# A two-layer mixer kernel: where the inverse root of the latent key norm is turned into a column

## The reference, cut to what matters

```python
def _mla(c_q, c_kv, k_rope, positions, q_norm, kv_norm, wq_up, wkv_up, q_gain, k_gain):
    """c_q: (B,S,Q_RANK), c_kv: (B,S,KV_RANK), k_rope: (B,S,MLA_ROPE) shared over heads."""
    b, s, _ = c_q.shape
    q = (_rms_norm(c_q, q_norm) @ wq_up).reshape(b, s, MLA_HEADS, MLA_QK)
    kv = (_rms_norm(c_kv, kv_norm) @ wkv_up).reshape(b, s, MLA_HEADS, MLA_NOPE + MLA_V)
    k_nope, v = kv[..., :MLA_NOPE], kv[..., MLA_NOPE:]
...
    k = _rms_norm(k, k_gain).transpose(0, 2, 1, 3)
...
    return _from_heads(_causal_softmax_attention(q, k, v, MLA_QK ** -0.5))
...
def second_block(x, positions, ffn1_norm, ffn1_wi, ffn1_wo, mix_norm, w_in, b_in, ml_conv_w, ml_conv_b,
...
    for l in range(DEPTH_2):
        x = x + 0.5 * _swiglu(_rms_norm(x, ffn1_norm[l]), ffn1_wi[l], ffn1_wo[l])

        u = _rms_norm(x, mix_norm[l])
        c = _split_cols(u @ w_in[l] + b_in[l])
...
        y_mla = _mla(c['mla_cq'], c['mla_ckv'], c['mla_kr'], positions, mla_q_norm[l], mla_kv_norm[l],
                     mla_wq_up[l], mla_wkv_up[l], mla_q_gain[l], mla_k_gain[l])
...
        x = x + merged @ w_out[l]

        x = x + 0.5 * _swiglu(_rms_norm(x, ffn2_norm[l]), ffn2_wi[l], ffn2_wo[l])
    return x
```

## Time and profile before

| | |
|---|---|
| median of 3 runs | 2370.8 us (2369.12 to 2372.78) |
| the profiled execution | 2373.44 us |
| its span (first to last instruction) | 2371.6 us |
| PE busy | 2350.4 us, 99% of the span |
| PE in the chain that ended last | 97% of the span |
| mean granted TensorE clock | 0.997 |
| DVE, ACT, POOL busy | 49%, 41%, 56% of the span |

### The profile page before, as it was taken

One profiled execution on the slowest core, in us unless ns is written; L12 is line 12 of the kernel. 1 busy time (PEld: TensorE's weight loads), 2 busy tenths in 40 slices (PEclk: granted clock), 3 DMA queues, 4 the chain that ended last, 5 costly groups with the idle time before them and its releaser, 6 DMA issues.

```text
span 2371.6 us, 29650 instructions
## 1 busy us (share of the span) xinstructions
PE 2350.4 (99%) x11116; PEld 1917.7 (81%) x11116; DVE 1161.2 (49%) x1812; ACT 982.1 (41%) x1561; POOL 1319.6 (56%) x1589
## 2 busy tenths in 40 slices
PE   8999999999999999999999999999999999999999
PEld 8777788888888888777888888888887778888887
DVE  5895475422324432479636733333325795366330
ACT  4555644222223233566534432332346655343321
POOL 5784256655656654457345755555554573466554
PEclk9999999999999999999999999999999999999999
DMA  4322133333333333222132333333332122233333
GB/s 159 103 80 72 40 94 98 98 97 98 92 97 111 98 98 96 73 70 80 54 89 80 98 98 98 98 92 99 95 96 80 54 81 62 81 89 98 98 98 98
DMA packets 60862, 212.88 MB, mean 90 GB/s; under 512 B 6704, under 2 KB 8112, under 8 KB 60720
## 3 DMA queue, kind: packets, MB, share of 16 engines
q1 hardware_dynamic: 60576, 210.86, 29.5%
q10 hardware_dynamic: 144, 0.14, 0.0%
HBM read 208.87 MB, written 2.10 MB: 89 GB/s over the span
## 4 chain that ended last, share of the span: by engine, by line
PE 97%; ACT 1%; issue 1%; DVE 1%; POOL 0%; DMA 0%; SPq 0%; DVEq 0%
PE banks L741 96%; PE banks L1030 0%; PE banks L860 0%; POOL t L2046 0%; DMA t<-in_w 0%; ACT t L1715 0%; PE banks L910 0%; ACT t L1779 0%; PE banks L1087 0%; ACT t L1748 0%; ACT L2007 0%; ACT t L1751 0%; ACT t L1928 0%; ACT t L1746 0%; DVE t L1523 0%
## 5 line engine op out<-in xcount | busy, mean ns | idle before, releaser
L741 PE MATMUL banks<-t,t 128*128 128x512 f32 (+9 forms) x10836 | 2327.6, 386 | 18.1 <-ACT t L1735 5.8
L741 PEld LDWEIGHTS banks<-t,t 128*128 128x128 f32 (+2 forms) x10836 | 1886.6, 188 | 438.1 <-issue 51.5
L2046 POOL TENSOR_TENSOR t<-t,t 128x256 fp32r<-128x256 f32 x1544 | 1262.9, 849 | 1021.5 <-ACT t L1715 1012.7
L1715 ACT ACTIVATE t<-t 128x1024 fp32r<-128x1024 f32 x385 | 407.8, 1060 | 1075.7 <-issue 617.9
L1233 DVE TENSOR_TENSOR t<-banks,t 128x512 f32<-128x512 f32 x121 | 83.1, 687 | 171.3 <-PE banks L741 169.2
L1400 DVE TENSOR_TENSOR t<-banks,t 128x512 f32<-128x512 f32 x44 | 30.4, 691 | 184.1 <-PE banks L741 183.9
L1368 DVE SCALAR_TENSOR_TENSOR t<-banks,t 128x512 f32<-128x512 f32 x32 | 22.1, 692 | 155.4 <-PE banks L741 155.4
L1116 DVE SCALAR_TENSOR_TENSOR t<-t,t,t 128x512 fp32r<-128x512 f32 x64 | 52.9, 831 | 57.4 <-ACT t L1735 57.3
L1345 DVE TENSOR_TENSOR t<-t,t 128x512 fp32r<-128x512 f32 x68 | 70.1, 1031 | 2.3
L1735 ACT ACTIVATE t<-t,t 128x512 fp32r<-128x512 f32 x64 | 45.6, 715 | 55.6 <-DVE t L1368 49.1
L1374 DVE TENSOR_TENSOR t<-banks,t 128x512 f32<-128x512 f32 x24 | 16.6, 692 | 106.0 <-PE banks L741 106.0
(11 more groups left out here) (186 smaller groups left out, 1258.5 us busy)
## 6 DMA issues: line engine op xcount, KB each, us to landing
t<-in_w SPq DMA_DIRECT2D x386, 512.0 KB, 3.5
t<-in_xT SPq DMA_DIRECT2D x8, 256.0 KB, 6.0
out<-t SPq DMA_DIRECT2D x8, 256.0 KB, 4.4
t<-in_vbias SPq DMA_DIRECT2D x2, 384.0 KB, 4.0
t<-in_c SPq DMA_DIRECT2D x1, 576.0 KB, 8.4
t<-in_w SPq DMA_DIRECT2D x2, 256.0 KB, 4.0
t<-in_pos SPq DMA_DIRECT2D x2, 256.0 KB, 3.7
t<-in_dmask SPq DMA_DIRECT2D x4, 128.0 KB, 4.4
```

Of the source, the lines that this page charges most:

```text
L741: return pe.matmul(o, l, r, start=start, stop=stop, skip_group_check=True)
L1715: a.activation(whl[u % 2][:, 0:1024], wraw[u % 3][:, :], ACT.Copy).then_inc(*w_high.next(u))
L2046: p.tensor_tensor(hl[:, 1024:2048][:, c], wraw[u % 3][:, c], as_f32(hl[:, c]), ALU.subtract).then_inc(*w_low.next((u, q)))
```

## The change

The four thin matmuls of `cols` and their copy are taken out of `low_item`, where they followed the inverse roots, and are emitted between the last `qup` and the first `vup`. Instead of a bank of the item's own pair they take the next of the two banks of the dense products, so that the products behind them have the other bank of the two than before. `low_item` is done, for `until`, one step earlier. What is computed is the same.

```diff
                 put("low_sums", l)
                 yield "a", (t_attn, ("low_kv", l))
                 put("low_rs", l)
-                yield "t", (v_attn, ("low_kv", l))
-                put("cols", ("low", l), pair(slot)[0], 0, RKV, natural, rcol_t[:, 4:8], (v_attn, ("low_kv", l)))
                 sch.done.add(("low", l))
...
                 sch.pump()
+            put("cols", ("low", l), sch.bank(), 0, RKV, natural, rcol_t[:, 4:8], (v_attn, ("low_kv", l)))
             for t_ in range(2):
                 b = sch.bank()
                 g = len(groups)
```

## The result

The changed kernel takes 2378.36 us in the median of nine runs (2374.06 to 2379.40), the kernel before, run beside it, 2371.46 us (2367.62 to 2375.78). The ratio is 1.0027, with a 95% interval from 1.0019 to 1.0035: 6.4 us slower, a little over what a measurement of this kernel can tell from no change. The forecast was 4.0 us slower, and the likeliest class in it was "the same".

The account below looks back on a forecast made before the run. PE, busy 2350.4 of 2371.6 us, was taken to bound the kernel. Freed wait 0, thin matmuls 1.82, clock 2.2 and moved attention steps 0 made 4.0 us on 2370.8: 2374.8, range 2371.4 to 2378.2.

Parts of the forecast that it names:

- the same: Class of outcome: a time between 2366.1 and 2375.5 us, not told from no change; chance 0.66.
- The freed wait: Removing the wait behind line 1138 ahead of `kup` gains 0; at most 2.06 us a layer if the chain did not hold.
- The thin matmuls at the values: Four thin matmuls a layer ahead of `vup`, in PE's running stream, add 0.91 us a layer, 1.82 in all.
- The clock: At PE's restart the clock falls in both layers in nearly every run; 2.2 us in the first, 0 in the second.
- The attention steps among the gate products: Moved steps in the mixer, same matmuls and no PE wait: 0, half a microsecond a layer either way.
- The sum: For the whole kernel, 1.82 + 2.2 = 4.0 us, put on the median 2370.8: 2374.8.
- slower: Class of outcome: a time from 2375.5 us up; chance 0.32.
- second case: Clock at the restart as before, only the thin matmuls' cost left: 2372.6 us, chance 0.23.
- The clock does as it did: Rival: clock at the restart falls as often as before, only the thin matmuls cost, 1.8 us: 2372.6; chance 0.23.
- the early keys pay: Rival: the earlier `kup` pulls its successors forward, both waits of 2.06 us go: 2368.5; chance 0.05.
- The clock falls at the values too: Rival: thin and narrow matmuls at the values lower the clock, 1.7 us a layer more: 2378.2; chance 0.17.

Follow-up runs that it names:

- e1: The kernel before, its order kept, with the thin matmuls and their copy left out: 2373.92 us, ratio 1.0010.
- e3: The changed kernel with 12 unread 512-column matmuls behind the first key projection, in PE's long wait: 2374.26 us, ratio 1.0008 to the kernel before.
- e2: The kernel before with the thin matmuls and copy moved ahead of the values, banks exchanged, all else in its old order: 2375.41 us, ratio 1.0018.
- e9: The kernel before with 16 unread full fp32 128x128 matmuls in one block in each mixer's last gate products: 2380.27 us, ratio 1.0039.
- e10: The kernel before with 16 unread full fp32 128x128 matmuls a layer, one behind each of 16 gate steps: 2377.96 us, ratio 1.0031.
- e11: As e10, but each spare matmul writes 64 output rows in place of 128: 2391.02 us in a single run, beside 2375.2 for the kernel before.
- e4: The kernel before with 8 unread matmuls a layer ahead of the thin ones, in the wait behind line 1138: 2369.59 us, ratio 0.9990.

## Why the prediction was right or wrong

**The freed wait: right.** It forecast a gain of 0, because `mlk`'s evacuation on DVE and ACT sets the restart. In the changed kernel the wait moved to line 1233 with 6.6 us, and the restart is 4.43 us behind the start of line 1138 as before; e1, which has only the removal, is not faster. From the end of `mlk`, three matmuls of 0.23 us ahead of 1055.47, to the restart at 1060.55 it is 5.8 us, where it said 5.7.

**The thin matmuls at the values: right.** 0.91 us a layer was forecast; 0.89 is what e3 shows at full clock against the earlier trace rows, and e2 stands 1.5 to 1.9 us over e1. No wait for a bank came, and the copy fits in DVE's hole.

**The clock: right in kind, and about right in size.** It falls in both layers, as forecast, behind what the forecast named: the first `kup` has left the stretch ahead of the restart, and three matmuls are left in it. The thin matmuls left that stretch too, and no run parts the two. What the Trainium skill says in "TensorE: Matmul & The Clock Gate", section "HAM oscillation — how this bites in real kernels", that matmuls in short bursts between waits run on a slow clock, agrees with both layers here, where the trace of before agreed in one. In the page's own kernel the waits are for DMA; here they are for DVE, 3.31 us the longest. The term was 2.2 us. The runs' mean time at half clock rose from 10.2 to 15.8 us. A fall of 3.41 us cost 1.42 us at the restart and 1.5 at the values of e3, one of 6.83 cost 2.73: some 0.4 of the length each time. So 5.6 us more make an estimated 2.3 us, give or take half a microsecond for the rounding alone. By places, the profile alone would mislead: the first layer lost 1.42 us to its new fall (13.36 - 11.04 - 0.9), and the second gained about as much, since its fall was 3.41 us long instead of the 6.83 of the earlier trace rows.

**The attention steps among the gate products: wrong.** This is the step that failed. It said 0, half a microsecond a layer either way, because the matmuls are the same and PE has no wait there. It is 0.85 a layer, 1.7 in all, outside its own bounds. The flaw was to take "no wait" for "no cost". In these traces the step from one matmul to the next depends on the shapes of both, and the new order breaks a block of 64-row matmuls in two. Such borders account for 0.33 of the 0.85 us; for the rest, the three longer steps between 512-column matmuls among it, the cause is open.

**The sum.** 1.8 + 1.7 + 2.3 = 5.8 us, against 6.4 measured (4.5 to 8.3 by the interval) and 4.0 forecast. Of the missing 2.4 us, 1.7 are the order; the remaining 0.7 can't be told from noise. At the same recorded clock (0.999, 0.997, 0.996) the changed kernel's runs stand 3.6, 4.3 and 5.3 us above the mean of the kernel before beside e1, where the thin matmuls and the order alone make 3.5. The kernel lies just past the bound at which slower begins, in the class that had a chance of 0.32. Its median is 0.2 us above the range as stated, which ended at 2378.2; counted from the 2370.8 us that the forecast started from, 6.4 us more is 2377.2, inside it. (The range's low end, 2371.4, is 1.2 us under its second case, not the one microsecond named there.)

**The rivals.** "The clock does as it did" is refuted by e1 and e3 together; "the early keys pay" by e1. "The clock falls at the values too" can happen: e3's profile has it in both layers. But it is not needed for the changed kernel's loss: its profile has no fall there, and e1, with nothing put in at the values, spends as long at half clock (16.4 us). It isn't excluded for every run either. Five of the nine runs read a clock of 0.996, under the profiled one's 0.997, and where their further falls lie isn't on record. That its total of 2378.2 came so near is luck.

## What to carry to other kernels

A wait that the table names is only the last of those that stand in line; before taking it away, follow the chain of waits one step further, to what would be late next. Matmuls that sat in a wait were free here, and helped to hold the clock up: moving them into a running stream cost their full length, and without them the clock fell at the old place. When an edit lets a planner reorder what follows, compare a long stretch of the two traces from one fixed point to another, since the engine can lose time there without any wait.

## What the runs showed of the hardware

A change between rounded-halves matmuls of 512 columns and full fp32 ones of 128, both with 128 output rows, cost 0.01 us there and back (e9, e10). Going over to a 64-row output and back cost 0.45 us among 512-column matmuls (e11), four times the 0.11 us of the small matmul itself.

The clock fell in e3 at 1069.24 with PE busy all through the stretch ahead of it; there the records were of one and of 128 columns, but for one of 512. And the cure was cheap: eight matmuls for nothing in each layer, where PE waits anyway, were worth 0.0010 of the time, with an interval of 0.0001 to 0.0019 (e4).

The clock is a good part of the spread of this kernel. Of its 33 runs beside e1, those with a mean clock of 1.000, 0.999, 0.998 and 0.997 took 2367.9, 2370.4, 2371.9 and 2373.6 us in mean, those with 0.996 2373.0; the groups overlap. Of the ten beside e9, the seven with 0.999 or more took 2368.9 to 2370.7 us, and the three with 0.997 or 0.998 took 2373.1 to 2374.2.
